# Four column strips and a 66-column root for seven RMS norms of a decoder step in fp32

## The reference, cut to what matters

```
def rms_norm(x, g):
    y = x * lax.rsqrt(jnp.mean(x * x, axis=-1, keepdims=True) + EPS)
    return y * g

sh, sc, gt = ada_mod(c, w, b)                 # silu(c) @ w + b, three parts of 1024
h = rms_norm(x, g_pre) * (1 + sc) + sh        # norm before a sublayer
f = sublayer(h)
x = x + gt * rms_norm(f, g_post)              # norm after it, gate times block, residual
```

## Time and profile before

| | us |
|---|---|
| median of 3 runs | 1779.47 (1777.6 to 1786.41) |
| profiled execution, its time | 1784.68 |
| profiled execution, its span | 1782.8 |
| PE busy | 1614.7 (91%) |
| DVE busy | 1251.4 (70%) |
| ACT busy | 982.8 (55%) |

### The profile page before, as it was taken

One profiled execution on the slowest core, in us unless ns is written; L12 is line 12 of the kernel. 1 busy time (PEld: TensorE's weight loads), 2 busy tenths in 40 slices (PEclk: granted clock), 3 DMA queues, 4 the chain that ended last, 5 costly groups with the idle time before them and its releaser, 6 DMA issues.

```text
span 1782.8 us, 22939 instructions
## 1 busy us (share of the span) xinstructions
PE 1614.7 (91%) x8712; PEld 1317.8 (74%) x8712; DVE 1251.4 (70%) x1092; ACT 982.8 (55%) x881; POOL 134.9 (8%) x130
## 2 busy tenths in 40 slices
PE   5869999799898767779999999999999999999992
PEld 3449999598785546458888888888888888888881
DVE  2455544478882352348888888888888888888884
ACT  1144433333322232247787787777777777777772
POOL 0000000015540220110000000000000000000001
PEclk9589999999999557769999999999999999999996
DMA  9965546755468111949999999999999999999982
GB/s 322 362 215 166 183 154 203 254 199 174 160 230 309 58 29 66 357 164 357 380 359 393 377 370 379 376 382 375 367 393 382 371 382 368 382 375 374 386 299 86
DMA packets 249295, 513.45 MB, mean 288 GB/s; under 512 B 9977, under 2 KB 69545, under 8 KB 249217
## 3 DMA queue, kind: packets, MB, share of 16 engines
q1 hardware_dynamic: 243691, 492.49, 77.0%
q0 software_dynamic: 4768, 17.37, 2.5%
q10 hardware_dynamic: 766, 2.65, 0.4%
HBM read 498.58 MB, written 14.35 MB: 288 GB/s over the span
## 4 chain that ended last, share of the span: by engine, by line
PE 78%; DVE 11%; DMA 3%; POOL 3%; issue 2%; ACT 2%; SPq 0%; POOLq 0%; DVEq 0%; ACTq 0%
PE wide L477 22%; PE wide L478 22%; PE wide L479 22%; POOL phase L1789 2%; DVE phase L1493 2%; PE wide L526 1%; PE wide L910 1%; POOL phase L1795 1%; PE wide L758 1%; PE wide L537 1%; DVE w_lo L1717 1%; DMA ring<-in_ada_ffn_w 1%; DVE w_lo L393 1%; DMA ring<-in_cache_v 1%; PE wide L512 1%
## 5 line engine op out<-in xcount | busy, mean ns | idle before, releaser
L1717 DVE TENSOR_TENSOR w_lo<-ring,w_hi 128x2048 fp32r<-128x2048 f32 x336 | 768.2, 2291 | 117.1 <-ACT w_hi L1220 115.7
L1220 ACT ACTIVATE w_hi<-ring 128x2048 fp32r<-128x2048 f32 x336 | 643.4, 1919 | 212.5 <-PE wide L479 212.5
L477 PE MATMUL wide<-w_hi,xe_hi 128*128 128x512 f32 x896 | 355.9, 397 | 6.0 <-DVE xe_lo L1722 4.4
L479 PE MATMUL wide<-w_hi,xe_lo 128*128 128x512 f32 x896 | 350.5, 391 | 0.0
L478 PE MATMUL wide<-w_lo,xe_hi 128*128 128x512 f32 x896 | 350.0, 391 | 0.0
L477 PE MATMUL wide<-tHi,w_hi 128*128 128x264 f32 x672 | 198.3, 295 | 28.2 <-DVE mLo L1411 28.2
L478 PE MATMUL wide<-mLo,w_hi 128*128 128x264 f32 x736 | 212.2, 288 | 0.0
L393 DVE TENSOR_TENSOR w_lo<-ring,w_hi 128x2048 fp32r<-128x2048 f32 (+1 forms) x58 | 138.3, 2388 | 98.8 <-ACT w_hi L974 98.4
L477 PEld LDWEIGHTS wide<-w_hi,xe_hi 128*128 128x128 f32 x896 | 169.0, 189 | 44.0 <-DVE w_lo L1717 5.8
L479 PEld LDWEIGHTS wide<-w_hi,xe_lo 128*128 128x128 f32 x896 | 168.9, 188 | 36.2
L478 PEld LDWEIGHTS wide<-w_lo,xe_hi 128*128 128x128 f32 x896 | 169.2, 189 | 33.5
(11 more groups left out here) (276 smaller groups left out, 1749.4 us busy)
## 6 DMA issues: line engine op xcount, KB each, us to landing
ring<-in_moe_w SPq DMA_DIRECT2D x336, 1024.0 KB, 7.2
ring<-in_ffn_w SPq DMA_DIRECT2D x30, 1024.0 KB, 5.3
ring<-in_ada_mix_w SPq DMA_DIRECT2D x24, 1024.0 KB, 7.7
ring<-in_ada_ffn_w SPq DMA_DIRECT2D x24, 1024.0 KB, 14.2
ring<-in_w_q SPq DMA_DIRECT2D x12, 1024.0 KB, 7.9
ring<-in_cache_k SPq DMA_DIRECT2D x24, 512.0 KB, 4.9
ring<-in_cache_v SPq DMA_DIRECT2D x24, 512.0 KB, 6.5
ring<-in_w_kv SPq DMA_DIRECT2D x8, 1024.0 KB, 6.5
```

The costliest lines, as they stand in the source:

```text
L477: pe.matmul(out, a[0], b[0], start=start, stop=False, skip_group_check=True)
L479: return pe.matmul(out, a[1], b[0], start=False, stop=stop, skip_group_check=True)
L1220: act.activation(w_hi[:, (NSPLIT + k) % PAIRS, :], ring[:, slot, :], ACT.Copy).then_inc(hi_done, 1)
L1717: dve.tensor_tensor(w_lo[:, i, :], ring[:, slot, :], w_hi[:, i, :].bitcast(F32), ALU.subtract).then_inc(lo_done, 1)
```

## The change

Each norm's sums are made on four column strips of 32 weight columns, one strip for 66 tokens (`NQ`). Strip j writes the sums of tokens 66j to 66j+65 to partitions 32j to 32j+31 of bank 7, so that the root and the reciprocal work on 128x66. PE then spreads the result: four matmuls, each with column 32j of the identity broadcast to 128 columns as weights, write the 264 reciprocal roots to all partitions of bank 0. `normalise` reads them there, and PE's queue waits in `norm_sum` for the reciprocal. For norms 1, 3 and 5 a new function `gated` first makes gate times block into `hT`; `residual` then is one product with the spread reciprocal and one addition per half, over all 264 tokens. After norm 4 the spread reciprocal is copied to `rstd`, for `key_input`. DVE's wait for the mixer's transposes of `hT` (`ps_turned`) moves ahead of `gated(0, mT)`.

```
+NQ = NT // 4
+        std4, inv4 = std[:, 0:NQ], std[:, NQ:2 * NQ]
+        spread_rstd = bank[0][:, 0:NT]
 # PE, norm_sum
-                    mm = pe.matmul(bank[7][:, 0:NT], ones, tT[:, k, :], start=(k == 0), stop=(k == KC - 1))
+                    for j in range(4):
+                        mm = pe.matmul(bank[7][32 * j:32 * (j + 1), 0:NQ], ones[:, 0:32], tT[:, k, NQ * j:NQ * (j + 1)],
+                                       start=(k == 0), stop=(k == KC - 1))
                 mm.then_inc(norm_summed, 1)
+                pe.wait_ge(std_ready, i + 1)
+                for j in range(4):
+                    mm = pe.matmul(bank[0][:, NQ * j:NQ * (j + 1)], ident[:, 32 * j:32 * j + 1].to_broadcast([P, P]), inv4,
+                                   start=True, stop=True)
+                mm.then_inc(norm_spread, 1)
 # ACT, norm
-                act.activation(std[:, :], bank[7][:, 0:NT], ACT.Sqrt, bias=eps1, scale=1.0 / D).then_inc(std_ready, 1)
+                act.activation(std4, bank[7][:, 0:NQ], ACT.Sqrt, bias=eps1, scale=1.0 / D).then_inc(norm_root, 1)
 # DVE
             def inverse(i):
-                dve.wait_ge(std_ready, i + 1)
-                link(dve.reciprocal(rstd[:, :], std[:, :]))
+                dve.wait_ge(norm_root, i + 1)
+                dve.reciprocal(inv4, std4).then_inc(std_ready, 1)
+                dve.wait_ge(norm_spread, i + 1)
             def normalise(src, ks):
-                link(dve.tensor_tensor(tT[:, ks, :], src[:, ks, :], wide4(rstd[:, :]), ALU.mult))
+                link(dve.tensor_tensor(tT[:, ks, :], src[:, ks, :], wide4(spread_rstd), ALU.mult))
-            def residual(s, ks, done):
-                for k in range(ks.start, ks.stop):
-                    dve.scalar_tensor_tensor(xT[:, k, 0:T], tT[:, k, 0:T], ada[:, s, 16 + k, 0:1], xT[:, k, 0:T], ALU.mult, ALU.add)
-                link(dve.tensor_tensor(small[:, ks, :], tT[:, ks, T:NT], vec(s, 2, ks)[:, :, 1:9], ALU.mult))
-                link(dve.tensor_tensor(xT[:, ks, T:NT], xT[:, ks, T:NT], small[:, ks, :], ALU.add))
+            def gated(s, src):
+                for k in range(KC):
+                    dve.tensor_scalar(hT[:, k, 0:T], src[:, k, 0:T], ada[:, s, 16 + k, 0:1], None, ALU.mult)
+                link(dve.tensor_tensor(hT[:, :, T:NT], src[:, :, T:NT], vec(s, 2, slice(0, KC))[:, :, 1:9], ALU.mult))
+            def residual(ks, done):
+                normalise(hT, ks)
+                link(dve.tensor_tensor(xT[:, ks, :], xT[:, ks, :], tT[:, ks, :], ALU.add))
 # DVE, norms 1 and 2 (3 and 5 alike, without the moved wait)
+            dve.wait_ge(ps_turned, 1)
+            gated(0, mT)
             inverse(1)
             for ks in HALVES:
-                normalise(mT, ks)
-                residual(0, ks, norm_in)
+                residual(ks, norm_in)
             inverse(2)
-            dve.wait_ge(ps_turned, 1)
 # DVE, behind norm 4
+            dve.tensor_copy(rstd[:, :], spread_rstd)
```

More of the change, by code:

```diff
@@ L309, in yoco_step @@
         norm_in, sq_ready, norm_summed, std_ready = sem("norm_in"), sem("sq_ready"), sem("norm_summed"), sem("std_ready")
+        norm_root, norm_spread = sem("norm_root"), sem("norm_spread")
         h_ready = sem("h_ready")
@@ L1443, in _ @@
                 dve.sem_inc(norm_in, 1)
+            gated(1, mT)
             inverse(3)
-            for hf, ks in enumerate(HALVES):
-                normalise(mT, ks)
-                residual(1, ks, norm_in)
+            for ks in HALVES:
+                residual(ks, norm_in)
             i_lin, i_wo = firsts[("wq", 0)], firsts[("wo", 0)]
@@ L1627, in _ @@
                 dve.sem_inc(norm_in, 1)
+            gated(2, woT)
             inverse(5)
-            for hf, ks in enumerate(HALVES):
-                normalise(woT, ks)
-                residual(2, ks, norm_in)
+            for ks in HALVES:
+                residual(ks, norm_in)
             inverse(6)
```

## The result

| | before | changed |
|---|---|---|
| median, us (20 runs each) | 1777.86 (1769.76 to 1786.41) | 1785.33 (1780.66 to 1793.60) |
| profiled execution: time, span, mean clock | 1784.68, 1782.8, 0.928 | 1787.96, 1786.2, 0.923 |

The ratio is 1.0043 [1.0024, 1.0063]: some 7.5 us slower, less than the 0.5% that the prediction named as its limit, but outside its range of 1769 to 1784 and on the other side of no change. Rival 2's 1785 is hit almost to the microsecond, in part by luck: it had added 5.6 us to a median of 1779.47, and the change cost 7.5 on one of 1777.86.

The account below looks back on a forecast made before the run. PE, 78% of the chain, bounds the kernel, so only norms 1 to 4 in stages 1 and 2 count. Gains of 3.1 and 1.85 us make 5.0, giving 1774.5 us against a median of 1779.47; range 1769 to 1784.

Parts of the forecast that it names:

- Rival 2: PE's clock falls to 1.2 GHz around the norms; four slow products and columns behind norms 2 and 4 give 1785; chance 0.2.
- the price of 1.92 and 0.98 us: Modulation products and their columns behind the norms run at full speed; two of each behind norm 1 take 5.8 us.
- Sums: Norm sums on four strips take 1.0 us per half; in norms 1 and 3 they end after 2.05 us instead of 3.83.
- Rival 1: The strips give nothing: sums take 1.92 us a half, kernel 2.1 us slower, 1781.6; chance 0.1.
- Root, reciprocal, spread: From sums' end to normalise: 0.32, 0.57 and 1.05 us plus hand-overs, 2.2 instead of 2.39, gaining only 0.2 us.
- Residual: Norms 1 and 3, first half's normalise to second half's squares: 5.2 us instead of 6.82, gaining 1.6 a norm; PSUM reads free.
- Gate times block: Added 2.9 us on DVE ahead of the reciprocal, covered by its idle time; in stage 1 done at 92.9, root at 93.0.
- The wait's queue: PE waits in `norm_sum` for root, reciprocal and spread; modulation products begin 2.15 us behind the sums' end, not 0.07 ahead.
- Stage 3: No gain, as it waits for a slab; asking 0.6 us later costs between 0 and 0.6, taken as 0.
- Rival 3: Weights or the weight slab hold the next sublayer's start; 1.85 us or nothing is left, 1777.5 to 1779.5; chance 0.1.

Follow-up runs that it names:

- e1: Changed kernel with unread matmuls filling PE's pauses ahead of and behind the sums of norms 1 to 6; 1774.01 us, 0.9991 of the kernel before.
- f2: Changed kernel with two unread matmuls only behind each norm's sums, in PE's wait for the reciprocal; 1774.63 us, 0.9983 of the kernel before.
- e2: Kernel before with only its sums made short, squares and ones in fp32r, no spread, no wait; 1777.80 us, ratio 1.0001.
- e3: Kernel before with only gate times block (`gated`) and the shorter `residual`; 1777.48 us, ratio 1.0005.
- f1: Changed kernel with PE's reciprocal wait and spread behind the next product, plus unread matmuls ahead of the sums; 1770.64 us, 0.9960 of the kernel before.
- e4: Changed kernel with PE's reciprocal wait and spread moved behind the next modulation product; 1773.63 us, 0.9977 of the kernel before.
- f4: Kernel before with only PE waiting behind each norm's sums until DVE's reciprocal is done; 1791.47 us, ratio 1.0066.

## Why the prediction was wrong

**The step that failed** is rival 2's "Against: stages 1 and 2 ran without such slow products before", and with it the price of 1.92 and 0.98 us for products and columns behind the change. The two products and columns behind norm 1 were to take 5.8 us and took 7.4 (94.23 to 101.64); the product and columns behind norm 2 were to take 3.87 and took 7.15 (106.92 to 114.07). Full speed was taken as a property of the stages; by e1, f2 and e2 it hung on the work that the change takes away and on the pauses that it leaves. A row in hand showed that the clock can fall around a norm: 728 to 730 us, 0.79, behind a pause of PE. But it could not say when it would; the same pause ahead of the same sums stood in stage 1 of that profile, at full speed:

```profile
101.34 2.05 PE L537 MATMUL wide<-tT,const 128*128 128x264 f32 x8 [1.22 <-ACT tT L998]
...
728.48 3.25 PE L537 MATMUL wide<-tT,const 128*128 128x264 f32 x8 [1.22 <-ACT tT L998]
```

Rival 2 had the right mechanism and a chance of 0.2; by the runs it should have been the forecast. "The gain of 5.0 is gone from two such on" held: five products over 3 us stood in the two stages. Its sum of 10.6 us came near the 13.8 measured, but for other records: it counted four products behind norms 2 and 4, of which two were slow, and none behind norms 1 and 3, where three were.

The other steps, one by one:

- **Sums**: 1.0 us a half forecast, 0.67 measured; they ended 1.64 us behind their start instead of 2.05. Rival 1 (1.92) falls. The 32 records of a half took 21 ns each, or 42 ns for each of its 16 matmuls. By the Trainium skill ("TensorE: Matmul & The Clock Gate", part 1) some 62 ns go on each matmul when hardware decode is off. That rule did not bind here, and the prediction's 2.0 us had also counted records for matmuls.
- **Root, reciprocal, spread**: 0.32, 0.57 and 1.05 forecast; 0.32, 0.57 and 1.11 measured at full speed. From the sums' end (92.08) to normalise (94.34) 2.26 us, forecast 2.2. What was missed is that the spread itself can run at half speed: 1.97.
- **Residual**: 5.2 us forecast; 94.34 to 99.58, 5.24. The product from PSUM took 1.25, so reading there cost nothing. But ACT squared only at 101.21, since it copies the second product's row first, which the half-speed product had made late: 11.89 us behind the first square of norm 1, against 10.25 in e1 (97.69 - 87.44).
- **Gate times block**: covered. It was done at 92.13, forecast 92.9, and DVE still waited 0.44 for the root.
- **The wait's queue**: in e1, which keeps it at full clock, the stages gain 3.3 and 1.7 against 3.1 and 1.85: 5.1 in sum, forecast 5.0. Stage 3's +0.4 in e1 lies within the 0 to 0.6 allowed.
- **Stage 3**: in the changed kernel it too had two products of 3.6 us, but ended no later against its start (-0.6), since the kernel before waited for a slab and made its last columns at half speed too (3.59). The 7.7 us that the prediction held against the slab's 17 are the median of the other two matrices' slabs; the page gives 14.2 for those of stages 1 and 3.
- **Rival 3** falls: from `ada_take` to the sublayer's first product it took 12.67 us (126.84 - 114.17), before 124.47 - 111.80 = 12.67; in stage 2 8.27 against 8.26. In e1, where `ada_take` did come earlier, it is 12.68 and 8.27.

**Open**: e1's stages gain 5.1 us but its median 3.1 and its ratio 1.6 (interval 4.3 of gain to 1.1 of loss). e3 has the same gap: its three stages gain 2.4, its ratio loses 0.9. For f1, e4 and f2 stages and ratio agree (7.6 and 7.1, 4.4 and 4.1, 3.0 and 3.0). The stretch from `ada_take` of stage 2 to norm 5 took 358 to 362 us in the profiles of nine of these kernels and 367 in that of the kernel before, at a granted clock of 0.83 to 0.86; one profile of each doesn't tell whether that spread has anything to do with the change. What decides whether a given pause lets the clock fall is open too: f4 has six alike, and two slow products.

## What to carry to other kernels

Before shortening what PE does between two waits, or giving PE a wait, look at the granted clock of the stretch and price the matmuls behind it at both levels: here 5 us of true savings met 13.8 us of half-speed matmuls. Where a short wait of PE can't be avoided, put useful work into it (a product that is due anyway, e4 and f1) or matmuls whose result nobody reads (e1). And judge such an edit by the clock and time of its stage as well as by the whole, since the whole's runs of the kernel before spread over 17 us; more than one profile of each would be better still.

## What was not expected of the hardware

- No pause of PE in stage 1 of the changed kernel, from the sums of norm 1 to the slow product, was longer than 1.11 us, and still the product at 94.23 ran at half speed; sets of 32 records in 0.67 us lay between the pauses. Two unread matmuls, 1.16 us together, in place of one such pause kept it at 1.92 (f2).
- Unread matmuls more than paid for themselves: stage 1 of e1 has 14 records more than that of the changed kernel, some 4.0 us of PE work in its pauses, and became 5.9 us shorter.
